# Softmax attention: both pieces of a unit's scores ahead of the transposes of the unit two back

## What is computed

```python
def diff_attention(q1, q2, k1, k2, v, lam):
    s1 = jnp.einsum('bqhd,bkhd->bhqk', q1, k1).astype(jnp.float32) * ATTN_SCALE
    s2 = jnp.einsum('bqhd,bkhd->bhqk', q2, k2).astype(jnp.float32) * ATTN_SCALE
    w = jax.nn.softmax(s1, axis=-1) - lam * jax.nn.softmax(s2, axis=-1)
    return jnp.einsum('bhqk,bkhe->bqhe', w, v.astype(jnp.float32))
```

## Time and profile before

| what | value |
|---|---|
| median of 3 runs | 3732.4 us |
| lowest and highest | 3731.8 and 3734.17 us |
| profiled execution, its own time | 3732.36 us |
| span of its instructions | 3730.4 us |
| mean granted clock of TensorE | 0.954 |
| context units, from and to | about 543 to 590 us of the span |
| da and wa units, first and last scores | 590.60 and 1008 us |

### The profile page before, as it was taken

The page is one execution under the profiler, slowest core; times in us unless marked ns, Lnnn a source line. Parts: engine busy times, 40 slices in busy tenths (PEclk is TensorE's granted clock), DMA queues, the critical chain, the costliest instruction groups (busy, mean ns, idle before and its releaser), DMA issues. The chain is left out here.

```text
span 3730.4 us, 52592 instructions
## 1 busy us (share of the span) xinstructions
PE 3377.7 (91%) x21774; PEld 2899.0 (78%) x21774; DVE 1628.8 (44%) x2517; ACT 1226.5 (33%) x2230; POOL 260.4 (7%) x332
## 2 busy tenths in 40 slices
PE   7899978999878999897999998887888899999998
PEld 2699976666667999875888995556766799999777
DVE  2306725555565112165526104553555455444343
ACT  3212325555564234124524103443332211111232
POOL 2000000000011000111211100001110000000010
PEclk9899989999988999998999998998998899999999
DMA  9224550000053222233321212001003111111332
GB/s 329 85 83 148 157 186 24 12 12 12 12 209 129 74 75 75 89 104 136 108 51 41 86 39 62 12 1 7 2 2 114 63 45 45 50 46 34 124 125 95
DMA packets 196721, 289.30 MB, mean 78 GB/s; under 512 B 41606, under 2 KB 137670, under 8 KB 194480
## 3 DMA queue, kind: packets, MB, share of 16 engines
q1 hardware_dynamic: 176624, 216.90, 18.0%
q0 software_dynamic: 19904, 69.65, 5.7%
HBM read 217.60 MB, written 68.90 MB: 77 GB/s over the span
## 5 line engine op out<-in xcount | busy, mean ns | idle before, releaser
L115 PE MATMUL p_pb<-p_w_hi,h_hi 128*128 128x416 f32 (+2 forms) x1216 | 424.7, 349 | 6.9 <-DVE p_w_lo L110 6.9
L117 PE MATMUL p_pb<-p_w_hi,h_lo 128*128 128x416 f32 (+2 forms) x1216 | 421.8, 347 | 0.0
L116 PE MATMUL p_pb<-p_w_lo,h_hi 128*128 128x416 f32 (+2 forms) x1216 | 419.6, 345 | 0.0
L115 PE MATMUL fu_pf<-h_hi,fu_w_hi 128*128 128x344 f32 (+1 forms) x1056 | 339.3, 321 | 8.7 <-DVE fu_pf L3422 8.7
L116 PE MATMUL fu_pf<-h_lo,fu_w_hi 128*128 128x344 f32 (+1 forms) x1056 | 340.2, 322 | 0.0
L117 PE MATMUL fu_pf<-h_hi,fu_w_lo 128*128 128x344 f32 (+1 forms) x1056 | 338.8, 321 | 0.0
L115 PEld LDWEIGHTS p_pb<-p_w_hi,h_hi 128*128 128x128 f32 x1216 | 229.0, 188 | 16.0 <-issue 14.6
L116 PEld LDWEIGHTS p_pb<-p_w_lo,h_hi 128*128 128x128 f32 x1216 | 229.2, 188 | 1.9
L117 PEld LDWEIGHTS p_pb<-p_w_hi,h_lo 128*128 128x128 f32 x1216 | 228.9, 188 | 0.7
L115 PEld LDWEIGHTS fu_pf<-h_hi,fu_w_hi 128*128 128x128 f32 x1056 | 199.7, 189 | 9.1 <-DVE fu_pf L3422 9.1
L117 PEld LDWEIGHTS fu_pf<-h_hi,fu_w_lo 128*128 128x128 f32 x1056 | 199.6, 189 | 0.0
(11 more groups left out here) (521 smaller groups left out, 7174.7 us busy)
## 6 DMA issues: line engine op xcount, KB each, us to landing
mod_w<-in_adaln_w SPq DMA_DIRECT2D x12, 2048.0 KB, 16.0
fu_raw<-in_ffn_up SPq DMA_DIRECT2D x88, 256.0 KB, 3.1
fd_raw<-in_ffn_down SPq DMA_DIRECT2D x44, 512.0 KB, 3.6
la_qkv<-p SPq DMA_DIRECT2D x16, 1024.0 KB, 5.0
p<-p_o SPq DMA_DIRECT2D x60, 208.0 KB, 1.9
s_raw<-in_w_in POOLq DMA_DIRECT2D x48, 256.0 KB, 3.5
rT<-p_stage SPq DMA_DIRECT2D x10, 896.0 KB, 4.8
p_raw<-in_ab_w_in POOLq DMA_DIRECT2D x10, 832.0 KB, 6.8
```

What stands on the lines that cost most here:

```text
L115: pe.matmul(out, left[0], right[0], start=start, stop=False)
L116: pe.matmul(out, left[0], right[1], start=False, stop=False)
L117: return pe.matmul(out, left[1], right[0], start=False, stop=stop)
```

## The change

In each round of PE, `score(u, 1)` is issued right behind `score(u, 0)`. Before, the wait for the exponentials of unit u - 2 (`weighed`) and its first transposes, `turn(u - 2, 0)`, stood between the two. No instruction is added or taken away, and the other engines' lists are the same.

```diff
--- before.py
+++ after.py
@@ -1139,12 +1139,10 @@
                         if units[u] == ("da", 2, 0):
                             pe.wait_ge(q1_in, 16)
                         score(u, 0)
+                        score(u, 1)
                     if u >= 2:
                         weighed(u - 2)
                         turn(u - 2, 0)
-                    if u < NU:
-                        score(u, 1)
-                    if u >= 2:
                         if u - 2 == 6:
                             pe.wait_ge(vb_in, 16)
                         if u - 2 == 7:
```

## The result

| | before | changed |
|---|---|---|
| median | 3733.28 us (4 runs) | 3776.28 us (4 runs) |
| lowest and highest | 3731.8 and 3747.48 us | 3772.02 and 3786.32 us |
| profiled execution | 3732.36 us | 3772.02 us |
| span | 3730.4 us | 3770.1 us |

The ratio is 1.0105, with a 95% interval of 1.0076 to 1.0133. The forecast was 3774.5 us, in a range of 3763 to 3790.

A forecast was written before the change was run, and what follows sets the result against it. Bound: a chain through PE's transposes and ACT's third copy to the exponentials, not the maxima. Da 0.56 plus wa 0.80 is 1.36 us a pair; 31 pairs give 42 us on 3732.4, so 3774.5 us, range 3763 to 3790.

The forecast's parts named there:

- the 0.0 us of ACT's idle time ahead of the exponentials: Ahead of 62 da exponentials ACT was never idle, so it does not wait for maxima, which are about 0.3 us early.
- Joined scores: In a da unit, all scores issued together ahead of turn 0: 2.35 us, against 2.55 for the two pieces apart.
- turn 1: Second transposes of a da unit: 3.69 us behind its first score, after 2.35 of scores and 1.34 around the copy.
- 0.80 was the sum: In a wa unit, the second score piece, two mode switches and a slower turn 0 add 0.80 us; bounds 0.53 to 0.90.
- The extra 0.1 us: In a wa unit, the second piece's last product waits for the mask products: taken as 0, with 0.1 us allowed.
- the half-price rival: Turn 1 or the copies recover part of the price: 1.03 us a pair or less, 3750 to 3765 us, 8%.
- The first pair: Left out, so 31 of 32 pairs count: it follows short context units with two copies, where the maxima do bind.
- The new wait: PE's weight loads wait for ACT's copy ahead of turn 1: new in da units, 0.8 to 0.9 us in wa units.
- The faster one: At the start of the exponentials, the maxima ended last: earlier scores gain 39 us, giving 3693.5 us, 3%.
- That the clock would fall more often: In the attention pairs, every third pair hit by a lower clock, ten more, adds 16 us: 3790 us, 12%.
- the one on tiling modes: Changing tiling mode drains the engine; the change removes two in each da unit, within the 0.20 us saved by joining.
- the one on rotating PSUM banks: Independent groups should rotate through PSUM banks so one's copy overlaps the next's products; for pT, speaks against the change.

The follow-up runs named there:

- dve_late_before: The kernel before the change, with one added VectorE operation of about 0.85 us between scores and maxima of every da and wa unit; 3789.04 us, ratio 1.0138.
- dve_late_after: The changed kernel with the same VectorE operation of about 0.85 us ahead of every maximum of a da and wa unit; 3779.07 us, ratio 1.0111.
- joined_da: The changed kernel with only da units having both score pieces ahead of the first transposes, wa units in the order of before; 3767.86 us, ratio 1.0083.
- joined_wa: The changed kernel with only wa units having both score pieces ahead of the first transposes, da units in the order of before; 3771.79 us, ratio 1.0084.
- first_and_two: The kernel before; in wa rounds first transposes ahead of scores, second in pS1, third directly behind; 3709.36 us, in more rounds 3715.87 us.
- turn_first_both: The kernel before, with the first transposes ahead of all scores in da and wa rounds; 3730.27 us, ratio 0.9974.

## Why the prediction was right

- **What binds.** The step that carried everything was the 0.0 us of ACT's idle time ahead of the exponentials: the copies end last, the maxima have 0.3 us to spare. `dve_late_before` measured that slack (0.88 us of delay cost 0.59 a unit on average), `dve_late_after` showed that it has grown to more than 0.88.
- **The da unit.** Joined scores were put at 2.35 us and took 2.35 (804.82 to 807.17); turn 1 was put at 3.69 and came at 3.69; 0.56 us later, as in `joined_da`.
- **The wa unit.** 0.80 was the sum; 0.80 (`joined_wa`) and 0.79 (the changed kernel, 6.39 to 7.18 us from its first score to the next da scores) were measured. The extra 0.1 us allowed for the wait on the mask products didn't show: the second piece's last product starts 0.43 us behind its first as before.
- **A pair** was put at 14.45 us and took 14.44, so nothing of the price was recovered and the half-price rival did not hold. The first pair was left out of the sum and grew by 0.03 us.
- **The new wait.** PE's weight loads were to wait 0.8 to 0.9 us for ACT's copy in wa units; they wait 0.92 us in both units, PE's transposes 0.69. The new idle time of PE is thus two times 0.69 us in a pair, not two times 0.9; the sum does not rest on this figure.
- **The rivals.** The faster one would need maxima that bind; they do, without an added operation, only once the transposes stop waiting (`first_and_two`), so its condition was named rightly. That the clock would fall more often did not come true here: once, and once again in the second profile, against two and none before, although PE is busy for a smaller share of a pair (11.88 of 14.44 us, not 11.87 of 13.10). The falls that this rival feared exist, though: they came where the waits ahead of the scores grew (`dve_late_before`), which the change left alone.
- **The time.** 3776.28 against 3774.5 us. That two hits in the pair give a hit in the total is partly luck: the later stage moves single runs by 20 us, which I had not in the sum. A range of 3763 to 3790 held all four runs, but for reasons that I hadn't listed.

The trace agrees with two rules of the Trainium skill that the prediction names. For the one on tiling modes in the Trainium skill ("TensorEngine Tiling (Array Packing)", "Key Properties"), joining the pieces of a da unit saved 0.20 us for two mode changes; how much of it is the change of mode, and how much the start of a second piece, no run separates. For the one on rotating PSUM banks in the Trainium skill ("Perfetto Trace Analysis", "Optimizing Tensor Performance"), a second place for one group of transposes took 0.39 us from the wa unit, and 1.35 us together with the earlier third transposes.

## What to carry to other kernels

Between two uses of a single buffer, whatever the other engine does with it is a hole: fill it with independent work (here the second piece of scores) or give it a second buffer, and do not queue the two uses back to back. A second buffer alone gave 0.39 us here, and 1.35 once the work behind it no longer waited for the same copy. Before moving work to make a result come earlier, look at what its reader waits for last: an engine that is never idle ahead of an instruction isn't waiting for its operands, and getting these sooner buys nothing. Where a program runs the same round many times, judge an edit by the length of a round in the trace; stages elsewhere can scatter by more than the edit is worth.

## What was not expected of the hardware

The clock of TensorE. A stage that no edit touches ran at a mean granted clock of 0.87 to 0.96 in different executions of one kernel and took 276.5 to 298.8 us, which moves the whole kernel by 0.6%. And in the first attention longer waits of PE ahead of the scores (1.31 us instead of 0.74 in da units, 1.03 instead of 0.44 in wa units) went with a clock that fell to 1.2 GHz in 10 of 31 pairs instead of 0 to 2, each time at a cost of about 1.6 us, while 0.69 us of new idle time in two other places of the round did nothing of the kind. In `turn_first_both`, with one wait of 1.05 us ahead of the da unit, it fell five times. Each of these counts is from one or two profiles. Which of the two waits matters, why idle time in the other places does not, and what decides it in the later stage, was not tried.
